# A ring of eight gathers for ten, and a weight tile that stays where it is

## What is computed

```
def peer_ffn(h, w_q, sub_keys, u, v):
    q = (ht @ w_q).reshape(T, PEER_HEADS, 2, PEER_DKEY // 2)
    s = jnp.einsum('thpc,hpnc->thpn', q, sub_keys, preferred_element_type=jnp.float32)
    v1, i1 = lax.top_k(s[:, :, 0], K)
    v2, i2 = lax.top_k(s[:, :, 1], K)
...
    top_s, pos = lax.top_k(cand, K)
    idx = jnp.take_along_axis(cand_idx, pos, axis=-1)
    g = jax.nn.softmax(top_s, axis=-1)
...
        ue = jnp.take(u, ib, axis=0)
        a = jnp.einsum('thkd,td->thk', ue, xb, preferred_element_type=jnp.float32)
        w = jax.nn.gelu(a) * gb
        ve = jnp.take(v, ib, axis=0)
        return jnp.einsum('thk,thkd->td', w.astype(ve.dtype), ve)
```

## Time and profile before

| | us |
|---|---|
| median of 3 runs | 1333.63 |
| lowest and highest of them | 1331.32, 1333.91 |
| profiled execution, its own time | 1332.32 |
| span of its instructions | 1330.5 |
| first gather issued, last gather issued | 247.0, 905.7 |

### The profile page before, as it was taken

The page is one execution under the profiler, slowest core; times in us unless marked ns, Lnnn a source line. Parts: engine busy times, 40 slices in busy tenths (PEclk is TensorE's granted clock), DMA queues, the critical chain, the costliest instruction groups (busy, mean ns, idle before and its releaser), DMA issues.

```text
span 1330.5 us, 12510 instructions
## 1 busy us (share of the span) xinstructions
PE 1211.0 (91%) x4454; PEld 730.4 (55%) x4454; DVE 791.2 (59%) x1886; ACT 231.9 (17%) x593; POOL 321.6 (24%) x276
## 2 busy tenths in 40 slices
PE   8999999988988887777988887688999899999998
PEld 7657996654554443333333333333466559888743
DVE  4667864589686887686877865655557932220001
ACT  2132210221111111113111112113102511000000
POOL 0100000334544544344445355541000000000000
PEclk9999999999999999799999899989999999999999
DMA  8531658799999999999999999998658534574540
GB/s 312 184 133 64 253 200 321 291 373 406 418 421 420 421 423 415 416 420 410 418 421 422 397 405 422 421 420 339 231 190 252 206 127 156 191 223 143 190 158 32
DMA packets 93789, 401.27 MB, mean 302 GB/s; under 512 B 6496, under 2 KB 9952, under 8 KB 60832
## 3 DMA queue, kind: packets, MB, share of 16 engines
q0 software_dynamic: 37440, 270.30, 49.3%
q1 hardware_dynamic: 56288, 130.18, 27.5%
HBM read 399.39 MB, written 1.06 MB: 301 GB/s over the span
## 4 chain that ended last, share of the span: by engine, by line
PE 60%; DMA 21%; DVE 14%; issue 2%; ACT 2%; POOL 1%; DVEq 0%; SPq 0%
DMA big<-in_peer_uv,idx_t 20%; PE ps L543 18%; PE ps L818 12%; PE ps L531 8%; DVE big L1941 6%; PE ps L1079 6%; PE ps L613 3%; PE ps L691 2%; PE ps L722 2%; PE ps L1041 2%; PE ps L749 2%; PE ps L591 1%; POOL big L1454 1%; DMA wring<-in_w_in 1%; ACT rows L1247 1%
## 5 line engine op out<-in xcount | busy, mean ns | idle before, releaser
L818 PE MATMUL ps<-big,rows 128*128 128x512 f32 x1024 | 482.4, 627 | 107.3 <-ACT rows L1247 107.2
L818 PEld LDWEIGHTS ps<-big,rows 128*128 128x128 f32 x1024 | 199.9, 200 | 371.8 <-issue 371.8
L1454 POOL DMA_INDIRECT big<-in_peer_uv,idx_t x256 | 310.3, 1212 | 377.3 <-PE ps L818 323.0
L1941 DVE CUSTOM_DVE_ANT_0 big<-big 128x1024 f32<-128x1024 f32 x256 | 307.9, 1226 | 139.6 <-DMA big<-in_peer_uv,idx_t 136.7
L543 PE MATMUL ps<-big,wring 128*128 128x256 f32 x1088 | 236.8, 379 | 0.0
L543 PEld LDWEIGHTS ps<-big,wring 128*128 128x128 f32 x1088 | 206.0, 190 | 28.0 <-issue 0.5
L531 PE MATMUL ps<-wring,big 128*128 128x512 f32 (+1 forms) x304 | 126.0, 571 | 0.0
L1241 ACT ACTIVATE small<-small 128x4 f32<-128x4 f32 (+2 forms) x68 | 13.9, 205 | 502.3 <-DVE small L1946 502.3
L531 PEld LDWEIGHTS ps<-wring,big 128*128 128x128 f32 x304 | 57.0, 190 | 62.8 <-issue 61.0
L1247 ACT ACTIVATE rows<-const,small 128x128 f32<-128x128 f32 x256 | 82.2, 390 | 21.1 <-DVE small L1950 21.1
L1079 PE MATMUL ps<-wring,big 128*128 128x512 f32 x176 | 75.7, 592 | 0.0
(11 more groups left out here) (287 smaller groups left out, 988.2 us busy)
## 6 DMA issues: line engine op xcount, KB each, us to landing
wring<-in_w_in SPq DMA_DIRECT2D x16, 2048.0 KB, 8.5
wring<-in_w_ada SPq DMA_DIRECT2D x10, 2048.0 KB, 7.9
wring<-in_w_gate SPq DMA_DIRECT2D x5, 2048.0 KB, 7.7
wring<-in_w_up SPq DMA_DIRECT2D x5, 2048.0 KB, 9.0
wring<-in_w_down SPq DMA_DIRECT2D x5, 2048.0 KB, 7.6
wring<-in_peer_wq SPq DMA_DIRECT2D x4, 2048.0 KB, 20.8
wring<-in_w_out SPq DMA_DIRECT2D x3, 2048.0 KB, 8.4
big<-in_peer_uv,idx_t POOLq DMA_INDIRECT x256, 13.0
```

The costliest lines, as they stand in the source:

```text
L818: last = nc.tensor.matmul(banks[h], diag[:, k % DIAGS, :], v_part[:, ring_at(k), h * 512:(h + 1) * 512], start=False, stop=(k % SLOTS == S ...
L1454: pool.indirect_dma_start(pair_ring[:, ring_at(k), :], None, a["peer_uv"], bass.IndirectOffsetOnAxis(idx_t[:, k:k + 1], 0))\
L1941: nc.vector.tensor_tensor_reduce(u_part[:, ring_at(k), :], u_part[:, ring_at(k), :], h_t[:, b, :], 1.0, 0.0, ALU.mult, ALU.add, a_dot[:, i ...
```

## The change

The ring has eight places for ten. The two places given up, 16384 to 20479 of `big`, stay the home of `peer_q1` for both blocks: its second load is gone from the list of tiles, and the query reads it there both times. No gather waits for the query of `peer_q1` any more. In the list the three tiles behind it, `ple_proj`, `ple0` and `ple1`, move up one place.

```
-RING, DIAGS, BATCH = 10, 8, 4
+RING, DIAGS, BATCH = 8, 8, 4
...
-    t += [(f"peer_q{i}", KD, 512, "peer_wq", 0, 512 * i) for i in (0, 2, 3, 1)]
+    t += [(f"peer_q{i}", KD, 512, "peer_wq", 0, 512 * i) for i in (0, 2, 3)]
...
             def query(name, b, parts=range(4)):
 
-                if (name, b) == ("peer_q1", 0):
+                if name == "peer_q1":
                     pe.wait_ge(q1_landed, 16)
                     wt = q1_home
...
                 if k < RING and ring_at(k) in (0, 6, 7):
                     wait_product(pool, "out1", 1)
-                if k < RING and ring_at(k) in (8, 9):
-                    wait_product(pool, "peer_q1", 0)
                 if k >= RING:
                     pool.wait_ge(pair_free, k - RING + 1)
```

## The result

The changed kernel took 1369.69 us, median of 4 runs (1364.19 to 1377.75), beside 1333.77 us of the kernel before (1331.32 to 1334.31): a ratio of 1.0278, interval 1.0221 to 1.0334. That is slower by 36 us, where 4.0 were predicted, and outside the range of 1330.7 to 1344.5. The profiled execution is the highest of the four, 1377.75 us with a span of 1376.0.

What follows compares the result with a forecast made beforehand. It took the gather stage as bound by DVE until about 325 us, then by full DMA engines. Terms -5.4 + 5.0 + 4.4 gave +4.0 us, a median of 1337.6 us, range 1330.7 to 1344.5.

Steps and rivals of the forecast that it cites:

- The bound: Stage of the gathers: DVE bounds from 263 to 325 us, then full DMA engines at 421 GB/s to its end.
- (a): Second load of `peer_q1`, 2.10 MB issued at 324.1 us in the full part, goes: -5.4 us.
- (b): `ple_proj`, `ple0` and `ple1` load earlier, all within the full part, with all bytes still moved: 0 us.
- (c): Gather 7 no longer waits for the query of `peer_q1` but lands as before behind queued transfers: 0 us.
- (d): Head start shrinks: two gathers less are done when the full part begins, +5.0 us (bounds 0 and 5.0).
- faster: Rival: one of two head-start gathers made up, late places covered; -2.9 us, 1330.7 us; chance 0.10.
- (e): Full part: transfers run dry where PE frees late as its clock falls; eight shortages, +4.4 us (bounds 0 and 10.3).
- the ring is too short: Rival: full-part lead is 6.2 us, or PE's clock falls more often; +9.9 us, 1343.5 us; chance 0.20.
- the late places are covered: Rival: full-part gathers behind others need less lead, 4.4 us, so shortages are 1.5; +1.1 us, 1334.7 us; chance 0.30.

Runs made afterwards that it cites:

- after_warm: The changed kernel with two more products on PE ahead of each batch from gather 192 to 243; 1366.23 us, 1.0228 to the kernel before.
- before_pairs: The kernel before, ten places, with batches of two instead of four from slot 192 on; 1334.86 us, ratio 1.0006.
- limit8_late: The kernel before, with at most eight of its ten places in use from gather 36 on; 1367.03 us, ratio 1.0247.

## Why the prediction failed, step by step

- **The bound** was read rightly: transfers, any pause one for one. The late part's loss went through to the end of the kernel in full: the last gather lands 46.6 us later in the profiled execution, and its span is 45.5 longer, so the tail is unchanged, as predicted.
- **(a)** The load: -5.4 predicted, -4.2 measured, the interval (-5.5 to -2.8) just reaches it. **(b), (c)** 0 predicted; (b) is inside the -4.2, (c) was not run alone, and the sum of the parts (35.2 for 35.9) leaves next to nothing over for it.
- **(d)** The head start: +5.0 predicted, +6.3 measured (+4.0 to +8.4). The mechanism was right. The rival "faster", in which one of the two gathers is made up and gather 35 lands near 353 us, did not come: it landed at 360.3.
- **(e)** The shortages: +4.4 predicted, +33.1 measured (+28.4 to +37.4). This is the failed step, and in it the sentence "What is needed: a lone gather into idle DMA engines took 5.3 us". The room was right: 7.2 us. The need was taken from a gather that had nothing ahead of it, "since it is the one landing measured with empty queues", but the question was how early a gather must go out for the transfers *not* to run empty. Room was counted to the last of the sixteen parts of the gather ahead, while the first engine is out of work some 2.1 us sooner. The 5.3 us of the lone gather and these 2.1 make an estimate of 7.4 us, beside the 7.5 to 8 of the table of leads; it is a rough one, as with the 3.8 us between the parts in the kernel before it would be 9.1. The same subtraction on the old trace gives 18.5 us with a need of 7.0, 27.3 with 7.5 (some 30 shortages), 38.3 with 8.0 (some 35). Measured are 33. The sum was steep just where the need lay, and the upper bound of 6.2 us was no bound: it was the lone figure with 0.9 more.
- The old trace held the answer close by. Gathers 15 and 18, the start and landing of each, before:

```profile
L1454 POOL DMA_INDIRECT big<-in_peer_uv,idx_t x1: 1305/1305/1305, 289.3 to 289.3; - x1
...
DMA to landing us min/median/max: 7.2/7.2/7.2
...
L1454 POOL DMA_INDIRECT big<-in_peer_uv,idx_t x1: 936/936/936, 297.1 to 297.1; - x1
...
DMA to landing us min/median/max: 8.1/8.1/8.1
```

  Gather 15 was issued 3.6 us before 14 landed, 18 was issued 4.4 us before 17 landed; they came 3.6 and 3.7 us after these, not 2.5. Transfers of 3.6 and 4.4 us still ahead, and still a gap over 1 us longer than the pace: the case that the new ring was in 38 times.
- The rival "the ring is too short" had the right name and the right side but stopped at a lead of 6.2 us and +9.9, where the leads that kept the pace were 7.5 to 8 us and the cost 33. It also named both mechanisms, lead and clock; after_warm shows the clock as the smaller. Its "against", that six of eight shortages are under half a us, held for that need alone: with 2.2 us more there are some 30 of them, six times as much in sum.
- The rival "the late places are covered" had the sign of the effect wrong: with transfers ahead the lead that was needed was longer here, not shorter. The page "DMA: Bandwidth & Descriptors" of the Trainium skill, its section on the anatomy of one SWDGE DMA, had spoken for it: its 2.0 us and the bytes over 436 GB/s give an estimate of 4.4 us. No trace here shows that; a lone gather took 5.3 and 5.4 us, and those with 1.5 to 5 us ahead 6.4 to 7.6 in the median of their group.
- The check it named for (e) was "gaps over 2.5 us between landings at the batches behind each fall of the clock and nowhere else"; wrong "if gaps stand at every batch (the room is less than I read)". What came lies between: of the 217 gaps from gather 37 on, 23 are over 3.5 us and 13 over 4, where the kernel before has one and none, and they remain where the clock is up (5 gaps over 3 us in after_warm, 6 in the changed kernel, between gathers 200 and 244). The room was as read; it was the need that was more.

## What to carry to other kernels

A ring's length is set by a loop: a batch is filled, it is used and its first place comes free, the next transfer is issued and lands. Add the three times as they are in flight and compare with ring length times pace. Near equality a place is worth either nothing or several per cent: here the tenth was worth nothing, the ninth 2.4% and the eighth 6%. The lead to put in is the shortest one in the trace with which the pace still held, not the time of a lone transfer. Where a transfer is split over several engines, look when the first of them runs out, not only when the last has landed. And where a ring can't be longer, release in smaller batches: that gave back a third of the loss here, in a part of the stage, and cost nothing with ten places (before_pairs).

## What was not expected of the hardware

- A gather of 1.05 MB issued with 3 to 5 us of gathers ahead of it lands 7.2 to 7.6 us after its issue and opens a gap of 3.3 to 3.8 us; only from about 5 us ahead (8.2 to landing) is the pace 2.5. The sixteen parts of a gather end some 2 us apart, and the rows of a new one begin 1.6 to 1.9 us after its issue; so the rate falls (213, 180, 246 GB/s in the windows above) before the last part ahead has landed. Why the first rows after a pause take up to 1.25 us instead of 0.31, why the parts lay 3.8 us apart before and 2.1 after, and why one part of gather 228 came 2.0 us behind the other fifteen, is open.
- The mean DMA share hides it: 0.97 in the full part with 8% less moved than at 1.01. A row that takes longer counts as busy for longer.
- The spread of the runs grew from 3.0 to 13.6 us. limit8_late shows the same (1359.94 to 1372.55), while with seven places it is 2.4 us. That a loop at its edge takes up each disturbance, where slack took it before, fits this but is not shown; each of the three has four runs.
